# A hybrid RWKV-7 / HGRN2 step: 14 of 16 row tiles of the HGRN input projection through seven products, chain and key copies reordered

## What is computed

```
q, f_logit, i, z = split(x @ w_in, 4)          # x: 544 x 2048, w_in: 2048 x 8192
f = lb + (1 - lb) * sigmoid(f_logit);  k = (1 - lb) * sigmoid(-f_logit)
q = silu(q) * 128 ** -0.5;  G = cumsum(log f)
o_t = sum over s <= t of (q_t . k_s * exp(G_t - G_s)) i_s  +  (q_t * exp(G_t)) @ S
S   = exp(G_last) * S + sum over s of (k_s * exp(G_last - G_s)) (x) i_s
out = (rmsnorm(o) * norm_w * silu(z)) @ w_o    # then x + rmsnorm(out)
```

## Time and profile before

| what | value |
|---|---|
| median of 3 runs | 2843.78 us (2841.17 to 2852.16) |
| the profiled execution | 2853.62 us, its span 2851.8 us |
| mean granted TensorE clock | 0.985 of full |
| PE busy | 2730.1 us, 96% |
| DVE, ACT, POOL busy | 1608.9, 1259.1, 138.4 us |
| first matmul of pair 0, of head 15's first dense tile | 1747.93, 2563.39 us |

### The profile page before, as it was taken

How to read it: one execution, slowest core, us unless ns; L and a number is a source line. 1 busy time by engine, 2 the same in 40 slices (tenths; PEclk the granted TensorE clock), 3 DMA queues, 4 the chain that set the end, 5 groups by cost and what they waited for, 6 DMA issues and landing times. The chain is left out here.

```text
span 2851.8 us, 82517 instructions
## 1 busy us (share of the span) xinstructions
PE 2730.1 (96%) x36816; PEld 2567.6 (90%) x36816; DVE 1608.9 (56%) x2679; ACT 1259.1 (44%) x1869; POOL 138.4 (5%) x116
## 2 busy tenths in 40 slices
PE   6999999999999999999889988999999999999997
PEld 5899999999998887888779978999999999999997
DVE  7335313313326777888742267776777767775224
ACT  5345323324414555555532255444544455444222
POOL 0000000000001111010000003000000000000000
PEclk8999999999999999999999999999999999999999
DMA  3333333333311111112132242222333223243322
GB/s 126 108 106 113 109 113 113 113 111 134 115 69 52 50 53 54 51 53 71 43 111 89 90 155 73 95 95 94 97 100 107 95 80 114 95 139 137 124 89 102
DMA packets 86816, 273.48 MB, mean 96 GB/s; under 512 B 16448, under 2 KB 29504, under 8 KB 65984
## 3 DMA queue, kind: packets, MB, share of 16 engines
q1 hardware_dynamic: 77248, 250.37, 26.5%
q10 hardware_dynamic: 9216, 17.83, 1.7%
HBM read 221.63 MB, written 46.54 MB: 94 GB/s over the span
## 5 line engine op out<-in xcount | busy, mean ns | idle before, releaser
L136 PE MATMUL w_pair<-a_x_hi,keep_w_hi 128*128 128x272 f32 x2016 | 428.4, 294 | 19.3 <-DVE a_x_lo L1059 18.5
L136 PE MATMUL w_pair<-a_x_lo,keep_w_hi 128*128 128x272 f32 x2016 | 419.7, 289 | 0.0
L136 PE MATMUL w_pair<-a_x_hi,keep_w_lo 128*128 128x272 f32 x2016 | 417.4, 288 | 0.0
L1045 DVE TENSOR_TENSOR keep_w_lo<-keep_raw,keep_w_hi 128x2048 fp32r<-128x2048 f32 x63 | 144.4, 2293 | 469.5 <-ACT keep_w_hi L798 469.5
L136 PEld LDWEIGHTS w_pair<-a_x_hi,keep_w_hi 128*128 128x128 f32 x2016 | 320.2, 189 | 25.7 <-issue 20.7
L136 PEld LDWEIGHTS w_pair<-a_x_lo,keep_w_hi 128*128 128x128 f32 x2016 | 318.1, 189 | 0.0
L136 PEld LDWEIGHTS w_pair<-a_x_hi,keep_w_lo 128*128 128x128 f32 x2016 | 317.8, 189 | 0.0
L136 PE MATMUL t_pair<-t_x_hi,keep_w_hi 128*128 128x272 f32 x1216 | 262.0, 297 | 18.2 <-DVE t_x_lo L2421 9.1
L136 PE MATMUL t_pair<-t_x_lo,keep_w_hi 128*128 128x272 f32 x1216 | 253.5, 290 | 0.0
L136 PE MATMUL t_pair<-t_x_hi,keep_w_lo 128*128 128x272 f32 x1216 | 253.3, 290 | 0.0
L812 ACT ACTIVATE a_stage<-w_pair 128x544 f32<-128x544 f32 x64 | 40.0, 625 | 425.1 <-PE w_pair L136 425.1
(11 more groups left out here) (448 smaller groups left out, 6146.7 us busy)
## 6 DMA issues: line engine op xcount, KB each, us to landing
keep_raw<-in_w_in SPq DMA_DIRECT2D x64, 1024.0 KB, 5.0
keep_raw<-in_hgrn_in SPq DMA_DIRECT2D x64, 1024.0 KB, 5.1
keep_raw<-in_rwkv_wo SPq DMA_DIRECT2D x16, 1024.0 KB, 5.0
keep_raw<-in_hgrn_wo SPq DMA_DIRECT2D x16, 1024.0 KB, 5.0
t_Ss<-in_hgrn_s SPq DMA_DIRECT2D x16, 512.0 KB, 7.1
out_hgrn_s<-t_Sd SPq DMA_DIRECT2D x16, 512.0 KB, 8.5
scr_r<-a_stage ACTq DMA_DIRECT2D x16, 272.0 KB, 2.2
scr_k<-a_stage ACTq DMA_DIRECT2D x16, 272.0 KB, 2.1
```

The costliest lines, as they stand in the source:

```text
L136: mm = pe.matmul(out[:, a, 0:TH], w, x[:, kt, a * TH:(a + 1) * TH], start=(kt == order[0] and n == 0), stop=(kt == order[-1] and n == 2))
L1045: dve.tensor_tensor(w_lo[b][:, :], raw[n % 2][:, :], w_hi[b][:, :].bitcast(F32), ALU.subtract).then_inc(p.raw_lo, 1)
```

## The change

`U` goes from 6 to 7: items are 128 x 896, rest columns 128 x 256, and a pair has 7 x 7 + 4 x 2 = 57 steps, 171 matmuls. S1 is no longer a tile of its own but is made in place in `raw[1]`, so the weight sums now run 3, 1, 2 in one go, at the end of a values pair for the next pair and behind `lower_first` in a values pair. In a gates pair DVE's `chain(e-1)` stands ahead of `weight_sum_4`, and ACT's `k_copy(e-1)` ahead of item 2. The step numbers of the head work are set anew, the norm's from 30 to 33. Under head 0 there is a seventh couple of row sums, levels and the key copy are placed ahead of several of the sums, the levels stand one step later in the dense tile, and PE's wait for the sums moves from the start of pair 0 to ahead of its product 2.

```diff
--- before.py
+++ after.py
@@ -37,7 +37,7 @@
 DECAY = float(np.exp(np.float32(-0.5)))
 RWKV_LEVELS = (1, 2, 4, 8, 16, 32)
 HGRN_LEVELS = (1, 2, 4, 8, 16, 32)
-U = 6
+U = 7
 UW = U * P
 CW = D - 2 * UW
 ITEMS = 7
@@ -1401,29 +1401,33 @@
         k = named(**tables)
...
@@ -1466,7 +1470,7 @@
             return slot[3] if (q, k) == (NQ - 1, ITEMS - 1) else slot[(ITEMS * q + k) % 3]
 
         def item_source(k):
-            return (raw[0][:, 0:UW], raw[0][:, UW:2 * UW], S2[:, :], S1[:, :], S3[:, :], S2[:, :], raw[1][:, UW:2 * UW])[k]
+            return (raw[0][:, 0:UW], raw[0][:, UW:2 * UW], S2[:, :], S1, S3[:, :], S2[:, :], raw[1][:, UW:2 * UW])[k]
 
         def weight_tile(g):
             if g < H0:
@@ -1681,7 +1685,6 @@
 
                 if q == 0:
                     pe.wait_ge(s.evac, GS - 1)
-                    pe.wait_ge(s.t_lo, 2 * U)
                 else:
                     pe.wait_ge(s.f0, q)
                 product(0, X, True)
@@ -1697,6 +1700,8 @@
                     pe.wait_ge(s.c12, q)
                 rest(0, 1, Z, True, s.c_used)
                 pe.wait_ge(s.p1, q + 1)
+                if q == 0:
+                    pe.wait_ge(s.t_lo, 2 * U)
                 product(2, X, False)
                 if q:
                     pe.wait_ge(s.evac, GS + 2 * q)
@@ -1875,11 +1880,11 @@
                 L = lambda m: (lambda: level(e, m))
                 keys = [lambda: k_by_token(e - 1), lambda: kv(e - 1)]
                 if 1 <= e < KT - 1:
-                    steps = dict(zip((13, 16, 18, 20, 22, 24, 27, 30), late(e - 1)))
+                    steps = dict(zip((18, 20, 22, 24, 26, 28, 30, 33), late(e - 1)))
                     if e > 1:
-                        steps.update(zip((3, 8), keys))
+                        steps.update(zip((3, 9), keys))
                     seven_products(2 * e - 2, steps)
-                    steps = {m: L(i) for i, m in enumerate((11, 14, 24, 31, 37, 42, 47, 51))}
+                    steps = {m: L(i) for i, m in enumerate((11, 16, 25, 31, 37, 42, 47, 51))}
                     seven_products(2 * e - 1, {**steps, 55: lambda: v_by_token(e)})
                     continue
                 if e:
@@ -1891,7 +1896,7 @@
                     dense(n + 3, dict(zip((1, 3, 6, 9, 12, 15), tail)))
                 else:
                     dense(n + 2, dict(zip((8, 9, 13), map(L, range(3)))))
-                    dense(n + 3, dict(zip((0, 3, 6, 7, 9, 11, 13, 15), [L(3), L(4)] + tail)))
+                    dense(n + 3, dict(zip((1, 4, 7, 8, 10, 12, 14, 15), [L(3), L(4)] + tail)))
             last = late(KT - 1)
 
             def sample_outs(first):
...
@@ -1989,6 +1996,8 @@
             def sums_hi(j):
                 even, odd = ((acc, zs), squares)[j % 2]
                 act.wait_ge(s.t_sum, 4 * j + 4)
+                if j in (3, 4):
+                    act.wait_ge(s.t_in, 2 * j + 4)
                 act.copy(T1[j][:, 0], even[:, half(0)]).then_inc(s.t_hi, 1)
                 act.copy(T42[j][:, :, 0], halves(odd[:, :])).then_inc(s.t_hi, 1)
 
@@ -2122,12 +2131,13 @@
             scaled_rows(0)
 
             def gates_pair(e, q):
+                if e > 1:
+                    k_copy(e - 1)
                 item_hi(q, 2)
                 if e > 1:
                     act.wait_ge(s.evac, H0 + 4 * e)
                     act.wait_ge(s.q1s, q)
                     silu(zs, s.zs)
-                    k_copy(e - 1)
                 for sem, count in ((s.q1, e), (s.kx, NUP * (e - 1) + 1), (s.qx, NUP * (e - 1) + 1), (s.ex, NUP * (e - 1) + 1)):
                     act.wait_ge(sem, count)
                 first_out(q, F)
@@ -2228,14 +2238,17 @@
                 level_out(e, 7)
                 if e == 0:
                     sums_hi(4)
-                    sums_hi(5)
                 if e == KT - 1:
                     for kt in range(4, 9):
                         high_part(2 * KT, kt, None)
                 k_copy(e)
                 if e < KT - 1:
-                    for j in range(U):
+                    sums_hi(5)
+                    scaled_rows(6)
+                    for j in range(U - 1):
                         third_sum_hi(j)
+                    sums_hi(U - 1)
+                    third_sum_hi(U - 1)
                     act.wait_ge(s.evac, n + 4)
                     silu(zs, s.zs)
             for kt in range(9, 11):
@@ -2324,28 +2337,26 @@
                 dve.tensor_tensor(c_lo[i][:, :], raw[i][:, 2 * UW:D], c_hi[i][:, :].bitcast(F32), ALU.subtract
                                   ).then_inc(s.c_lo, 1)
 
-            def weight_sum_1(q):
+            def weight_sum_3(q):
+                dve.wait_ge(raw_in[0], 16 * ((GS + 2 * q) // 2))
                 dve.wait_ge(raw_in[1], 16 * ((GS + 2 * q) // 2))
                 if q:
-                    dve.wait_ge(s.it_hi, ITEMS * (q - 1) + 4)
-                    dve.wait_ge(s.it_lo, ITEMS * (q - 1) + 4)
-                dve.tensor_tensor(S1[:, :], raw[1][:, 0:UW], raw[1][:, UW:2 * UW], ALU.add).then_inc(s.s1, 1)
+                    dve.wait_ge(s.it_hi, ITEMS * (q - 1) + 5)
+                    dve.wait_ge(s.it_lo, ITEMS * (q - 1) + 5)
+                else:
+                    dve.wait_ge(s.tile_ready, GS)
+                dve.tensor_tensor(S3[:, :], raw[0][:, 0:UW], S1, ALU.subtract).then_inc(s.s3, 1)
+
+            def weight_sum_1(q):
+                dve.wait_ge(s.s3, q + 1)
+                dve.tensor_tensor(S1, S1, raw[1][:, UW:2 * UW], ALU.add).then_inc(s.s1, 1)
 
             def weight_sum_2(q):
-                dve.wait_ge(raw_in[0], 16 * ((GS + 2 * q) // 2))
                 dve.wait_ge(s.s1, q + 1)
                 if q:
                     dve.wait_ge(s.it_hi, ITEMS * (q - 1) + 6)
                     dve.wait_ge(s.it_lo, ITEMS * (q - 1) + 6)
-                else:
-                    dve.wait_ge(s.tile_ready, GS)
-                dve.tensor_tensor(S2[:, :], S1[:, :], raw[0][:, 0:UW], ALU.subtract).then_inc(s.s2, 1)
-
-            def weight_sum_3(q):
-                if q:
-                    dve.wait_ge(s.it_hi, ITEMS * (q - 1) + 5)
-                    dve.wait_ge(s.it_lo, ITEMS * (q - 1) + 5)
-                dve.tensor_tensor(S3[:, :], raw[0][:, 0:UW], raw[1][:, 0:UW], ALU.subtract).then_inc(s.s3, 1)
+                dve.tensor_tensor(S2[:, :], S1, raw[0][:, 0:UW], ALU.subtract).then_inc(s.s2, 1)
 
             def weight_sum_4(q):
                 dve.wait_ge(s.it_hi, ITEMS * q + 3)
@@ -2523,6 +2534,8 @@
                 if e:
                     dve.wait_ge(s.o_mm, e)
                     dve.wait_ge(s.s_out, 16 * e)
+                else:
+                    dve.wait_ge(s.t3_lo, U)
                 dve.tensor_copy(S[0][:, :], blk(tok_ps, 0)).then_inc(s.S, 1)
                 for c in range(1, 4):
                     dve.wait_ge(s.S, 4 * e + c)
@@ -2548,12 +2561,11 @@
             def gates_pair(e, q):
                 if q:
                     lower_first(q - 1, zs)
-                weight_sum_3(q)
                 item_lo(q, 2)
+                if e > 1:
+                    chain(e - 1)
                 weight_sum_4(q)
                 item_lo(q, 3)
-                if e > 1:
-                    chain(e - 1)
                 item_lo(q, 4)
                 rest_lo(q, 1)
                 upper_first(q, F)
@@ -2571,14 +2583,14 @@
 
             def values_pair(e, q):
                 lower_first(q - 1, qr)
+                weight_sum_3(q)
                 weight_sum_1(q)
+                weight_sum_2(q)
                 first_q(e)
-                weight_sum_2(q)
                 item_lo(q, 2)
                 item_lo(q, 3)
                 take(e, 0)
                 widen(e, 0)
-                weight_sum_3(q)
                 weight_sum_4(q)
                 item_lo(q, 4)
                 take(e, 1)
@@ -2607,6 +2619,7 @@
                 widen(e, 6)
                 lower_second(q, zs)
                 if q < NQ - 1:
+                    weight_sum_3(q + 1)
                     weight_sum_1(q + 1)
                     weight_sum_2(q + 1)
 
@@ -2652,9 +2665,6 @@
                     sums_lo(1)
                 take(e, 3)
                 widen(e, 3)
-                if e == 0:
-                    sums_lo(2)
-                    item_lo(0, 0)
                 take(e, 4)
                 if e:
                     dve.wait_ge(s.vt_mm, e)
@@ -2662,21 +2672,27 @@
                     split_lo(n + 4)
                 widen(e, 4)
                 if e == 0:
-                    item_lo(0, 1)
-                    sums_lo(3)
+                    sums_lo(2)
+                    item_lo(0, 0)
                 take(e, 5)
                 widen(e, 5)
                 if e == 0:
+                    item_lo(0, 1)
+                if e == 0:
                     rest_lo(0, 0)
-                    weight_sum_1(0)
                 widen(e, 6)
                 if e < KT - 1:
+                    sums_lo(3)
                     sums_lo(4)
                     sums_lo(5)
```

(24 more changed lines are left out.)

## The result

The changed kernel took 2866.67 us (median, 2865.72 to 2866.83); the kernel before, run on the same chip, 2846.94. The ratio is 1.0066 [1.0049, 1.0084]; by it the change costs 18.8 us. The profiled execution took 2865.72 us, span 2863.8. Forecast were +20.8 us and 2864.6. The total came out as forecast, but by luck: two terms of its sum were wrong in opposite directions.

The account below looks back on a forecast made before the run. PE, busy 96%, was taken as the bound, with values pairs nearly full on DVE too. Double pairs +15.1 us and entry +5.7 us made +20.8 on 2843.78: 2864.6 us, range 2838 to 2873.

Parts of the forecast that it names:

- part 4: Values pair: three weight sums in a row delay item 2 and level 4; PE waits about 1.0 us per double pair.
- Part 1: Pairs on PE: 84 fewer matmuls save 0.75 us per double pair, the earlier key copy another 0.2.
- Part 2: Wider items: each 0.135 us more on DVE, 0.11 on ACT; DVE gets 1.9 us more per double pair.
- Part 3: Product 1 of values pairs: later norm and a chain 0.25 us longer make PE wait about 1.0 us.
- The alternative in part 4: Rest under GpSimd contention: if slowed in proportion to columns, 256 columns save another 0.8 us and level 4 doesn't wait.
- Part 5: Head 0 and entry: product 2 of pair 0 starts 3.0 us later; entry +5.7 us, bounds +2 and above +8.
- PE alone: Rival for the pairs: PE alone sets the time, no new waits, -13.4 us, total 2830 to 2834 us; chance 15%.
- Only the norm chain waits: Rival: values pair catches up behind product 1; +1 and +5.7 us, 2850.5 us; chance 25%.
- The load into raw[1] late by 0.5 us: Rival in each pair: the load lands too late for the sums, another 14 us, 2879 us; chance 7%.
- one sign of being wrong: Entry: the forecast counts as wrong if product 2 of pair 0 starts before 1758 us.

Follow-up runs that it names:

- experiment 1: Changed kernel with its eight late steps three earlier: 2855.27 us, ratio 1.0012; kernel before with its late steps three later: 2864.56 us, 1.0041.
- Experiment 7: Changed kernel with late steps three earlier and, in values pairs, weight sum 3 making only 128 of 896 columns: 2848.31 us, ratio 0.9998.
- experiment 4: Changed kernel with ACT's value copy for head 0 moved ahead of scaled_rows(5): 2867.64 us, ratio 1.0075.
- Experiment 3: Changed kernel with pair 0's weight sums ahead of the third sums on DVE, and z out before the state chain: 2863.97 us, ratio 1.0041.
- the first kernel of experiment 8: Changed kernel with late steps three earlier, DVE's entry sums and z reordered, S2 made from raw[1] minus S3, S1 last: 2840.27 us, ratio 0.9972.

## Why the prediction was right, and where not

The double pair can now be taken apart by runs. Fewer matmuls, with all waits gone: 57.27 - 58.35 = -1.08. DVE's queue of sums: 57.73 - 57.27 = +0.46. The norm's step: 58.87 - 57.73 = +1.14. Sum +0.52. In part 4's waits the forecast was 0.5 us too high, in the others within 0.15.

- **Part 1** (-0.75 and -0.2): right, -1.08 measured where the waits are away. The 0.13 us more were not taken apart.
- **Part 2**: right. Items take 1.09 us on DVE (0.953 + 0.135) and 0.94 on ACT (0.93).
- **Part 3** (chain +0.25, PE waits 1.0 us): right, +0.23 for the chain, 0.96 idle and 1.12 by distances for the wait, and by experiment 1 the cause. The chain is serial, so a later norm is paid for nearly in full.
- **Part 4** (1.0 us of waits): the mechanism was right, the size wrong; this is the term of the double pair that failed. Experiment 7 has 0.47 us in its place, at product 2 and level 4; levels 1 and 3 waited for nothing. From `lower_first` to the pair's end I had 26.14 going to 26.05. By the timelines, the stretch from `lower_first` to the values transpose went from 24.04 to 23.87 and one step fewer (0.377) follows it, so 25.6: 0.46 less than forecast. That is how much earlier `widen` 2 was ready than I had it (14.53 against 15.0). Of that, 0.1 is item 2's start; 0.16 is contention: GpSimd took 1.40 us from DVE (1.82 - 0.42) in place of 1.56; the rest was not taken apart. My 26.05 also doesn't follow from the 0.3 us that I name between `widen` 2 and level 4: it needs some 0.1, and 0.11 was measured.
- **The alternative in part 4** ("a slower rate in proportion to columns") failed as well. The rest, now 256 wide, took 0.40 us undisturbed, but the next operation with two SBUF inputs, as narrow, waited until 2033.18, 0.28 us past the end of GpSimd's at 2032.90. The contention moved on; the narrower operation didn't avoid it.
- **Part 5** (+5.7 us): the step that failed most, 10.8 us by the reckoning above and beyond its own upper bound of 8. Product 2 came 4.6 us later, not 3.0; that is 1.6. Beside the timelines of DVE, ACT and POOL my list starts 0.5 us too late (`sums_lo(3)` ends 27.0 us behind level 0, I had 27.6) and comes to 22.5 us, not 20.4. Of the 2.1 us more, 1.6 are the last weight sum, which I had at 1.1 us and which took 2.67 under GpSimd; each other item is within 0.2 us. The two waits ahead of it that I didn't foresee (5.29 and 2.49 us): the first costs next to nothing (experiment 4), the second wasn't tried alone. From product 2 to the start of pair 1 I had 2.7 us more than before, and it is 4.7. Experiment 3's kernel, at full clock there, has 2.6, so my term was right and the other 2.0 are the clock, which I named and left to the upper bound. Together they make the 9.24 us at the start of pair 1. The other 1.5 of the 10.8 are not the entry's. The 14 double pairs credit pair 0 with a gates pair's saving (0.68 us: 30.41 before, 29.73 after) that the 9.24 already hold, and my forecast made the same slip. The transpose stands at step 55 in both kernels, with one step less behind it after (0.38). And the last values pair takes 0.44 us longer up to it than the others (27.85 against 27.41), which it doesn't before.
- **Rivals.** PE alone: refuted by the 13.5 us of waits. Only the norm chain waits: nearest in the pairs (it gave +0.1 for a double pair; +0.52 measured), but by its own sign, `widen` 2 ready by 14 us, it isn't borne out (14.53). The load into raw[1] late by 0.5 us: neither PE nor DVE waits for a load in the pairs. ACT does, ahead of the cast of the rest (8.5 us in 13 waits, 3.9 in 6 before), but the first kernel of experiment 8 has 8.8 us of it and no wait of PE at product 1 or 2, so it costs nothing there.
- **Signs.** The double pair was forecast at 59.4 us and is 58.87. Product 0 of pair 0 starts 0.7 us earlier, not 2. By the letter one sign of being wrong came true: product 2 of pair 0 starts at 1757.40, before 1758. But level 0 came 5.6 us early by chance in that execution; counted from it, product 2 is 4.6 us late. A time from the span's start was the wrong sign to give.

So the total came out right by luck: 7.7 us too much in the pairs (15.1 forecast, 7.4 measured) met 5.1 too little at the entry (5.7 and 10.8), which makes 20.8 us forecast and 18.2 up to the last transpose.

## What to carry to other kernels

In a tuned kernel, ask for each shifted call on PE whether a serial chain of other engines hangs on it: three steps of shift cost 1.1 us in each double pair, more than the 0.75 forecast for the matmuls. Then the chain can be shortened where it is cheap; here the late steps where they were, DVE's sums of the entry in another order, and a sum written as a difference of what was already there turned +0.66% into -0.28 to -0.38%. Ask of the longest wait in a view who waits behind it: the edit against the 5.29 us one was worth 0.6 us, the edit against the 5.02 us one, last in the chain, 5.5. And price a long wait of PE with the slow matmuls that can follow it.
